# One weight preparation buffer, loaded and released in two halves of its columns

## The chip, the cores and the metric

The kernel runs on one core of a Trainium2 chip. The metric is the device time of one execution in microseconds; the kernel before took 2789.74 us (median of three runs). The engines are TensorE (PE, its weight loads shown as PEld), VectorE (DVE), ScalarE (ACT), GpSimd (POOL) and SyncE (SP), which issues most of the transfers.

## The reference

One layer of a hybrid decoder trunk over 2048 prompt tokens and 32 decoding tokens, in float32. Per token:

```
h = rmsnorm(x, g_mix_pre);  z = h @ w_in
a = z[value] * sigmoid(z[gate]) -> causal depthwise conv (31) -> group norm -> silu
hm = mlstm_chunkwise(q, k, v, i, f) -> per-head norm -> * sigmoid(z[o])
x = x + rmsnorm(concat(a, hm) @ w_out)
up = rmsnorm(x) @ w_up -> causal depthwise conv (3)
f = gelu(up[:, :D_FF]) * up[:, D_FF:]
x = x + rmsnorm(f @ w_down)
x = x + (p @ w_ple) * sigmoid(rmsnorm(x) @ w_ple_gate)
```

The model is 1024 wide, the feed-forward part 2816. The outputs are x and the states of the two convolutions and of the recurrence.

## The kernel before

The 2080 tokens are worked on in five blocks of 416. Features lie on the 128 partitions, tokens on the free dimension. Every product is made in three TensorE passes: a weight is kept as a high part (float32r) and a low part (the float32 value minus the high part), the activations likewise, and a 128x128 tile of weights costs `hi*hi`, `hi*lo` and `lo*hi` (lines 641 to 643), each 416 columns wide.

The weights are cut into 108 **units** of 128 x 1024 float32 values (512 KB). A unit serves 8 tiles, so 24 matmuls. In block 0 each unit is prepared once:

1. SP loads it raw into one of two buffers `w_raw[:, r % 2, :]` (`load_raw`, L522).
2. ACT copies it to the high part of `w[:, u % 3, 0, :]` (`high_part`, L1017). It does so inside its own fixed order of work, right after it has taken the result of the matmul group that used up unit u - 3 out of PSUM (`split_next`).
3. POOL subtracts to make the low part (`low_part`, L625). For 19 of the units VectorE does it (L2230, and L1808 for the first), in its own fixed order.
4. SP waits for that subtraction (`split_done`), loads the next raw unit but one into the buffer, and stores the finished pair of parts (1 MB) to the scratch tensor `w_kept` (`keep`, L529). The store must be complete before ACT writes that slot of `w` again (`s_kept`).

Blocks 1 to 4 only load finished pairs from `w_kept`; they have no raw loads, no copies and no POOL work. `w` is a ring of three slots, so TensorE can be at most two finished units ahead of the one in work. Each raw buffer has one counter `s_raw[i]` (a transfer adds 16), the high parts one counter `s_hi` (1 per unit), each slot of `w` one counter `s_w` (16 per unit, either from the subtraction or from a load).

Every engine runs a list of instructions in a fixed order. Around the change ACT's list for a pair j of up-projection groups in block 0 is: take group 2j out (L1398), split, GELU of pair j - 1 (L1406), take group 2j+1 out (L1398), split, high part of `f` for pair j - 1 (L1410). VectorE's is: `gated` (L2216), low part of `f` (L2220), the width-3 convolution of pair j (L2189, L2192), a copy of its tail (L2204), taps of the next block's width-31 convolution (L1722). The down projection (`f_split` as input) starts once the low parts of `f` are there. L1605 makes low parts of normalised activations, L1612 the scaled activations, L1600 sums squares, L2264 the low part of `p`, L806 begins a head of the recurrence after ACT's `columns` (L1126 to L1131).

Of the kernel before, what the change touches and what calls it, by code (L numbers as in the profile page):

```python
# [7 lines left out]
ALU = mybir.AluOpType  # L8
ACT = mybir.ActivationFunctionType
F32 = mybir.dt.float32  # L10
# [4 lines left out]
P = 128  # L15
D = 1024
KD = D // P
# [26 lines left out]
UNITS = 108  # L44
# [5 lines left out]
RAW = 2  # L50
RING = 3
# [104 lines left out]
def split_at(r):  # L156


    return SPLIT_UNITS[r]
# [26 lines left out]
def stores_before(u):  # L186


    return sum(split_at(r) % RING == u % RING and split_at(r) < u for r in range(SPLITS))
# [79 lines left out]
def hymba_layer(nc, t):  # L269
    ctx = ExitStack()  # L270
    with ctx:
# [3 lines left out]
        def signal(name, per, ring=0, unit=1):  # L275
            return Signal(ctx.enter_context(nc.semaphore(name)), per, ring, unit)
# [7 lines left out]
        w = sb("w_split", [P, RING, 2, KD * P], F32R)  # L284
        wg = sb("wg_split", [P, 2, KD, GATES], F32R)
        w_raw = sb("w_raw", [P, RAW, KD * P])
# [116 lines left out]
        s_setup = signal("s_setup", 0)  # L403
        s_ready = signal("s_ready", 0)
        s_gate_hi = signal("s_gate_hi", 0)
        s_raw = [signal(f"s_raw{i}", UNITS // RAW, unit=16) for i in range(RAW)]
        s_hi = signal("s_hi", UNITS)
        s_w = [signal(f"s_w{i}", UNITS // RING, unit=16) for i in range(RING)]
        s_kept = [signal(f"s_kept{i}", 0, unit=16) for i in range(RING)]
# [94 lines left out]
        def _(sp):  # L504
# [8 lines left out]
            def split_done(r):  # L513

                u = split_at(r)
                sp.wait_ge(s_w[u % RING].sem, s_w[u % RING].done(0, u // RING + 1))

            def load_raw(r):

                if r >= RAW:  # L520
                    split_done(r - RAW)
                sp.dma_start(w_raw[:, r % RAW, :], t["w_units"][source_of(split_at(r), False)]).then_inc(  # L522
                    s_raw[r % RAW].sem, 16)

            def keep(r):

# [91 lines left out]
        @block.gpsimd  # L618
        def _(pool):

            def low_part(n, r):

                slot = split_at(r) % RING
                pool.wait_ge(s_hi.sem, n + 1)
                nc.gpsimd.tensor_tensor(w[:, slot, 1, :], w_raw[:, r % RAW, :], w[:, slot, 0, :].bitcast(F32),  # L625
                                        ALU.subtract).then_inc(s_w[slot].sem, 16)

            for r in range(1, SPLITS):
                if r not in SPLIT_ON_VECTOR:
                    low_part(r, r)  # L630
# [374 lines left out]
        def _(act):  # L1005
# [5 lines left out]
            def high_part(u):  # L1011

                r = SPLIT_NTH[u]
                act.wait_ge(s_raw[r % RAW].sem, 16 * (r // RAW + 1))
                if u >= RING:
                    act.wait_ge(s_kept[u % RING].sem, 16 * stores_before(u))
                fn(w[:, u % RING, 0, :], w_raw[:, r % RAW, :], ACT.Copy).then_inc(s_hi.sem, 1)  # L1017

            def split_next(blk, split, g):

# [512 lines left out]
        def _(dve):  # L1533
# [22 lines left out]
            def program(blk, last, next_last=False, first=False, opening=False):  # L1556
# [247 lines left out]
                if first:  # L1804
                    sum_squares(0, range(KD))
                    inverse_root(0)
                    dve.wait_ge(s_hi.sem, 1)
                    v.tensor_tensor(w[:, 0, 1, :], w_raw[:, 0, :], w[:, 0, 0, :].bitcast(F32),  # L1808
                                    ALU.subtract).then_inc(s_w[0].sem, 16)
                    dve.wait_ge(s_rb.sem, s_rb.done(blk, 1))  # L1810
                    for i in range(KD + 4):
                        if i < KD:
# [410 lines left out]
                def low_part(u):  # L2223


                    if not opening or SPLIT_NTH.get(u) not in SPLIT_ON_VECTOR:
                        return
                    r, slot = SPLIT_NTH[u], u % RING
                    dve.wait_ge(s_hi.sem, r + 1)
                    v.tensor_tensor(w[:, slot, 1, :], w_raw[:, r % RAW, :], w[:, slot, 0, :].bitcast(F32),  # L2230
                                    ALU.subtract).then_inc(s_w[slot].sem, 16)

                def low_parts(g):
                    for u in USED_UP[False][g]:
# [212 lines left out]
```

## Time and profile before

| | |
|---|---|
| median of 3 runs | 2789.74 us (2786.82 to 2790.58) |
| the profiled execution | 2787.83 us, of which the traced span is 2785.8 us |
| PE, PEld busy | 97%, 94% of the span |
| DVE, ACT, POOL busy | 61%, 33%, 8% |
| mean granted TensorE clock | 0.994 of full speed |
| block 0 | about the first 665 us; all raw loads lie between 2.9 and 647.7 us |

A matmul takes about 350 ns from start to end but the next one starts about 189 ns later, since they are pipelined. So a busy PE of 97% hides small gaps; they are seen as idle time before a weight load (PEld). In the profile's tables the number in square brackets behind an instruction is the idle time of its engine just before it, with what ended it.

### The profile page before, as it was taken

How to read it: one execution, taken by the hardware profiler on the slowest of the kernel's cores; microseconds unless marked ns; L12 is line 12 of the kernel's file. 1: busy time of each engine (PE TensorE's matmuls, PEld its weight loads, DVE VectorE, ACT ScalarE, POOL GpSimd, SP SyncE). 2: the span in 40 equal slices, each digit the busy share in tenths (PEclk: the TensorE clock that was granted, in tenths of full speed). 3: DMA queues.
4: the chain of work that ended last, by engine and by line, in shares of the span. 5: the costliest groups of instructions: out<-in, count | busy, mean ns of one | idle time of the engine just before them, and what ended most of it. 6: DMA issues, size and time to landing. Idle time of an engine off the chain costs nothing.

```text
span 2785.8 us, 37566 instructions
## 1 busy us (share of the span) xinstructions
PE 2714.9 (97%) x14703; PEld 2610.3 (94%) x14703; DVE 1701.8 (61%) x3663; ACT 911.2 (33%) x1839; POOL 220.7 (8%) x92
## 2 busy tenths in 40 slices
PE   9989999999999999999999999999999999899998
PEld 7879999988899999999999999899999998799998
DVE  6976687765746756545566654656766636472644
ACT  5354433443532122434321223433112425211113
POOL 3421524311000000000000000000000000000000
PEclk9999999999999999999999999999999999999999
DMA  8747899978356666564666666556666576366665
GB/s 310 295 156 278 318 322 351 327 254 321 137 218 243 231 236 227 211 255 175 226 235 231 228 228 234 209 207 226 229 231 232 211 275 145 144 240 234 230 230 194
DMA packets 109562, 660.57 MB, mean 237 GB/s; under 512 B 20282, under 2 KB 20926, under 8 KB 39630
## 3 DMA queue, kind: packets, MB, share of 16 engines
q1 hardware_dynamic: 100238, 628.84, 63.2%
q10 hardware_dynamic: 9152, 29.36, 2.8%
q8 instruction: 117, 1.92, 0.3%
q14 instruction: 55, 0.45, 0.0%
HBM read 533.04 MB, written 125.11 MB: 236 GB/s over the span
## 4 chain that ended last, share of the span: by engine, by line
PE 77%; DMA 7%; DVE 7%; ACT 5%; POOL 2%; issue 1%; POOLq 0%; SPq 0%; DVEq 0%; ACTq 0%
PE proj L641 24%; PE proj L642 23%; PE proj L643 23%; DMA w_raw<-in_w_units 6%; POOL w_split L625 2%; ACT w_split L1017 2%; DVE mix_room L1600 1%; DVE small L1851 1%; DMA w_split<-w_kept 1%; PE m L679 1%; PE m L812 1%; DVE temp_room L1880 1%; PE m L818 1%; PE m L847 0%; PE m L848 0%
## 5 line engine op out<-in xcount | busy, mean ns | idle before, releaser
L641 PE MATMUL proj<-h_split,w_split 128*128 128x416 f32 x2720 | 977.8, 360 | 11.6 <-DVE h_split L1679 3.1
L642 PE MATMUL proj<-h_split,w_split 128*128 128x416 f32 x2720 | 954.0, 351 | 0.0
L643 PE MATMUL proj<-h_split,w_split 128*128 128x416 f32 x2720 | 948.4, 349 | 0.0
L641 PE MATMUL proj<-f_split,w_split 128*128 128x416 f32 x1568 | 566.0, 361 | 23.3 <-DVE f_split L1899 7.6
L642 PE MATMUL proj<-f_split,w_split 128*128 128x416 f32 x1568 | 553.7, 353 | 0.0
L643 PE MATMUL proj<-f_split,w_split 128*128 128x416 f32 x1568 | 550.1, 351 | 0.0
L641 PEld LDWEIGHTS proj<-h_split,w_split 128*128 128x128 f32 x2720 | 510.9, 188 | 25.6 <-issue 8.2
L643 PEld LDWEIGHTS proj<-h_split,w_split 128*128 128x128 f32 x2720 | 512.0, 188 | 8.7
L642 PEld LDWEIGHTS proj<-h_split,w_split 128*128 128x128 f32 x2720 | 512.5, 188 | 2.8 <-issue 1.0
L641 PEld LDWEIGHTS proj<-f_split,w_split 128*128 128x128 f32 x1568 | 297.1, 189 | 43.2 <-DVE f_split L1899 11.8
L643 PEld LDWEIGHTS proj<-f_split,w_split 128*128 128x128 f32 x1568 | 297.9, 190 | 5.3
L642 PEld LDWEIGHTS proj<-f_split,w_split 128*128 128x128 f32 x1568 | 298.0, 190 | 1.2
L1722 DVE SCALAR_TENSOR_TENSOR cv<-a_ext,vecs,cv 128x416 f32<-128x416 f32 (+1 forms) x480 | 289.7, 652 | 0.0
L2192 DVE SCALAR_TENSOR_TENSOR m<-temp_room,vecs,m 128x416 f32<-128x416 f32 (+1 forms) x440 | 256.8, 652 | 0.0
L625 POOL TENSOR_TENSOR w_split<-w_raw,w_split 128x1024 fp32r<-128x1024 f32 x88 | 220.5, 2507 | 436.4 <-ACT w_split L1017 436.4
L1398 ACT ACTIVATE temp_room<-proj 128x416 f32<-128x416 f32 x176 | 90.9, 517 | 470.7 <-PE proj L643 470.5
L2220 DVE TENSOR_TENSOR f_split<-m,f_split 128x416 fp32r<-128x416 f32 x110 | 65.1, 592 | 262.6 <-ACT f_split L1410 262.6
L2189 DVE TENSOR_SCALAR m<-temp_room,vecs 128x416 f32<-128x416 f32 (+1 forms) x220 | 146.1, 710 | 67.4 <-ACT temp_room L1398 66.5
L1017 ACT ACTIVATE w_split<-w_raw 128x1024 fp32r<-128x1024 f32 x108 | 114.1, 1057 | 145.3 <-DMA w_raw<-in_w_units 145.2
L1600 DVE TENSOR_TENSOR mix_room<-mix_room,temp_room 128x416 f32<-128x416 f32 x131 | 83.2, 635 | 109.5 <-ACT temp_room L1035 105.4
L1406 ACT ACTIVATE mix_room<-m 128x416 f32<-128x416 f32 (+1 forms) x110 | 57.2, 520 | 191.3 <-DVE m L2192 191.2
L1117 ACT ACTIVATE qkv<-proj 128x416 f32<-128x416 f32 x60 | 30.9, 515 | 167.8 <-PE proj L643 167.8
(284 smaller groups left out, 2226.1 us busy)
## 6 DMA issues: line engine op xcount, KB each, us to landing
w_split<-w_kept SPq DMA_DIRECT2D x432, 1024.0 KB, 4.8
w_kept<-w_split SPq DMA_DIRECT2D x108, 1024.0 KB, 7.7
w_raw<-in_w_units SPq DMA_DIRECT2D x108, 512.0 KB, 5.6
x_resid<-in_x ACTq DMA_DIRECT2D x5, 1664.0 KB, 12.5
out_y<-x_resid ACTq DMA_DIRECT2D x8, 832.0 KB, 8.9
rows<-in_x ACTq DMA_DIRECT2D x4, 832.0 KB, 8.2
w_raw<-in_x ACTq DMA_DIRECT2D x3, 832.0 KB, 11.9
qkv<-in_p ACTq DMA_DIRECT2D x5, 416.0 KB, 5.3
```

What stands on the lines that cost most here:

```text
L625: nc.gpsimd.tensor_tensor(w[:, slot, 1, :], w_raw[:, r % RAW, :], w[:, slot, 0, :].bitcast(F32), ALU.subtract).then_inc(s_w[slot].sem, 16)
L641: mm(dst, w_hi, a_hi, start=first, stop=False)
L642: mm(dst, w_hi, a_lo, start=False, stop=False)
L643: return mm(dst, w_lo, a_hi, start=False, stop=last)
L1017: fn(w[:, u % RING, 0, :], w_raw[:, r % RAW, :], ACT.Copy).then_inc(s_hi.sem, 1)
L1398: fn(s[:, n, 2:2 + T], src, ACT.Copy).then_inc(s_evac.sem, 1)
L1406: fn(gelu_out[:, j % 3, 0:wide], facc[j % 3][0][:, 0:wide], ACT.Gelu_apprx_tanh).then_inc(s_fgelu.sem, 1)
L1600: v.tensor_tensor(sq_sum, none if i == 1 else sq_sum, tile, ALU.add).then_inc(s_squse.sem, 2 if i == 1 else 1)
L1722: ins = v.scalar_tensor_tensor(acc[:, 0:n], a_ext[:, c, k:k + n], wt, acc[:, 0:n], ALU.mult, ALU.add)
L2189: ins = v.tensor_scalar(dst, src, wt, col("b_conv_ffn", n * FT + j), ALU.mult, ALU.add)
L2192: ins = v.scalar_tensor_tensor(dst, src, wt, dst, ALU.mult, ALU.add)
L2220: v.tensor_tensor(f[:, j % FH, 1, :], facc[j % 3][1][:, 0:T], f[:, j % FH, 0, :].bitcast(F32), ALU.subtract).then_inc(s_f.sem, 1)
```

## The change

The 1024 columns of a raw unit are treated as two halves of 512. Each half has its own load (256 KB), its own counter per raw buffer, its own ACT copy and its own subtraction on POOL or VectorE. A half of the raw buffer is loaded again once the subtraction of that half has been done: `s_w` now gets 8 from each half, and SP waits for the first 8 before the first half's load and for all 16 before the second's. The store of a finished unit and TensorE's wait for it still ask for both halves.

```diff
-        s_raw = [signal(f"s_raw{i}", UNITS // RAW, unit=16) for i in range(RAW)]
+        s_raw = [[signal(f"s_raw{i}_{part}", UNITS // RAW, unit=16) for part in range(2)] for i in range(RAW)]
+        raw_parts = (slice(0, KD * P // 2), slice(KD * P // 2, KD * P))
...
             def load_raw(r):
-                if r >= RAW:
-                    split_done(r - RAW)
-                sp.dma_start(w_raw[:, r % RAW, :], t["w_units"][source_of(split_at(r), False)]).then_inc(
-                    s_raw[r % RAW].sem, 16)
+                for part, cols in enumerate(raw_parts):
+                    if r >= RAW:
+                        u = split_at(r - RAW)
+                        sp.wait_ge(s_w[u % RING].sem, s_w[u % RING].done(0, u // RING + 1) - (0 if part else 8))
+                    sp.dma_start(w_raw[:, r % RAW, cols], t["w_units"][source_of(split_at(r), False)][:, cols]).then_inc(
+                        s_raw[r % RAW][part].sem, 16)
...
             def low_part(n, r):
                 slot = split_at(r) % RING
-                pool.wait_ge(s_hi.sem, n + 1)
-                nc.gpsimd.tensor_tensor(w[:, slot, 1, :], w_raw[:, r % RAW, :], w[:, slot, 0, :].bitcast(F32),
-                                        ALU.subtract).then_inc(s_w[slot].sem, 16)
+                for part, cols in enumerate(raw_parts):
+                    pool.wait_ge(s_hi.sem, 2 * n + part + 1)
+                    nc.gpsimd.tensor_tensor(w[:, slot, 1, cols], w_raw[:, r % RAW, cols], w[:, slot, 0, cols].bitcast(F32),
+                                            ALU.subtract).then_inc(s_w[slot].sem, 8)
...
             def high_part(u):
                 r = SPLIT_NTH[u]
-                act.wait_ge(s_raw[r % RAW].sem, 16 * (r // RAW + 1))
-                if u >= RING:
-                    act.wait_ge(s_kept[u % RING].sem, 16 * stores_before(u))
-                fn(w[:, u % RING, 0, :], w_raw[:, r % RAW, :], ACT.Copy).then_inc(s_hi.sem, 1)
+                for part, cols in enumerate(raw_parts):
+                    act.wait_ge(s_raw[r % RAW][part].sem, 16 * (r // RAW + 1))
+                    if u >= RING and part == 0:
+                        act.wait_ge(s_kept[u % RING].sem, 16 * stores_before(u))
+                    fn(w[:, u % RING, 0, cols], w_raw[:, r % RAW, cols], ACT.Copy).then_inc(s_hi.sem, 1)
```

The subtractions on VectorE (L1808, L2230) are split in the same way.

## Rows read from the trace of the kernel before

**Rows 1.** Instructions on the raw buffer, whole execution: count, ns min/median/max, first and last start.

```profile
L522 SPq DMA_DIRECT2D w_raw<-in_w_units x108: 327/333/718, 2.9 to 647.7; - x108
L1017 ACT ACTIVATE w_split<-w_raw x108: 1039/1060/1065, 10.9 to 653.6; 128x1024 fp32r<-128x1024 f32 x108
L625 POOL TENSOR_TENSOR w_split<-w_raw,w_split x88: 2357/2412/3934, 16.1 to 654.8; 128x1024 fp32r<-128x1024 f32 x88
...
L2230 DVE TENSOR_TENSOR w_split<-w_raw,w_split x19: 1215/1225/1233, 383.9 to 572.0; 128x1024 fp32r<-128x1024 f32 x19
...
  ACT w_split L1017: 145.2, 63
...
DMA to landing us min/median/max: 3.3/5.7/12.1
```

**Rows 2.** Chain that ended last, 320 to 340 us: start, length, what.

```profile
321.20 6.22 DMA w_raw<-in_w_units
...
327.45 1.07 ACT w_split L1017
...
328.65 2.42 POOL w_split L625
```

**Rows 3.** Busy time by stretch: two of block 0, one of a later block.

```profile
284.00:370.00 86.00, 85.60 (x451) 83.83 (x451) 55.91 (x96) 36.74 (x64) 44.42 (x18) 1.00 0.94 336
440.00:525.00 85.00, 84.84 (x447) 83.05 (x445) 60.09 (x98) 35.23 (x63) 43.48 (x19) 1.00 0.95 337
1000.00:1100.00 100.00, 99.95 (x530) 98.70 (x529) 63.59 (x122) 24.18 (x57) 0.00 (x0) 1.00 0.65 231
```

**Rows 4.** Weight loads with idle time before them, near the two down projections.

```profile
375.38 0.19 PEld L641 LDWEIGHTS proj<-f_split,w_split 128*128 128x128 f32 x1 [1.15 <-POOL w_split L625]
...
377.74 0.19 PEld L641 LDWEIGHTS proj<-f_split,w_split 128*128 128x128 f32 x1 [1.88 <-DVE f_split L2220]
...
525.42 0.19 PEld L641 LDWEIGHTS proj<-f_split,w_split 128*128 128x128 f32 x1 [0.68 <-issue]
...
532.77 0.19 PEld L641 LDWEIGHTS proj<-f_split,w_split 128*128 128x128 f32 x1 [2.32 <-DVE f_split L2220]
```

**Rows 5.** ACT in order of time, 375 to 377 us.

```profile
375.60 1.06 ACT L1017 ACTIVATE w_split<-w_raw 128x1024 fp32r<-128x1024 f32 x1 [1.99 <-DMA w_raw<-in_w_units]
376.56 0.50 ACT L1410 ACTIVATE f_split<-m 128x416 fp32r<-128x416 f32 x1
```

**Rows 6.** PE by stretch: busy, granted clock, DMA share, GB/s.

```profile
375.00:380.00 5.00, 3.10 (x12) 0.86 0.91 311
380.00:385.00 5.00, 5.00 (x23) 0.80 1.01 374
```

**Rows 7.** All engines in order of time, 267.9 to 270.9 us.

```profile
267.98 2.36 POOL L625 TENSOR_TENSOR w_split<-w_raw,w_split 128x1024 fp32r<-128x1024 f32 x1 [2.12 <-ACT w_split L1017]
...
268.09 2.70 DVE L1605 TENSOR_TENSOR h_split<-temp_room,h_split 128x416 fp32r<-128x416 f32 x1
...
270.84 0.19 PEld L641 LDWEIGHTS proj<-h_split,w_split 128*128 128x128 f32 x1 [2.22 <-DVE h_split L1605]
```

**Rows 8.** All engines in order of time, 605 to 609.4 us.

```profile
605.02 0.59 DVE L1600 TENSOR_TENSOR mix_room<-mix_room,temp_room 128x416 f32<-128x416 f32 x1
605.49 2.36 POOL L625 TENSOR_TENSOR w_split<-w_raw,w_split 128x1024 fp32r<-128x1024 f32 x1 [4.09 <-ACT w_split L1017]
...
605.82 2.48 DVE L1600 TENSOR_TENSOR mix_room<-mix_room,temp_room 128x416 f32<-128x416 f32 x1 [0.20 <-ACT temp_room L1035]
...
609.29 0.19 PEld L641 LDWEIGHTS proj<-f_split,w_split 128*128 128x128 f32 x1 [3.28 <-DVE f_split L2264]
```

**Rows 9.** ACT and PEld in order of time, 93 to 96.4 us.

```profile
93.19 1.06 ACT L1017 ACTIVATE w_split<-w_raw 128x1024 fp32r<-128x1024 f32 x1 [2.54 <-DMA w_raw<-in_w_units]
...
96.14 0.10 PEld L806 LDWEIGHTS m<-mask_b,sel_b 128*128 128x128 bf16 x1 [1.50 <-ACT small L1131]
```

**Rows 10.** DMA packets, 284 to 370 us and 1000 to 1100 us.

```profile
DMA packets 5284, 28.88 MB, mean 336 GB/s; under 512 B 591, under 2 KB 591, under 8 KB 2935
...
DMA packets 3173, 23.14 MB, mean 231 GB/s; under 512 B 352, under 2 KB 352, under 8 KB 352
```

**Rows 11.** Landing of the stores to `w_kept`, 280 to 540 us.

```profile
DMA to landing us min/median/max: 6.1/7.7/10.0
```

More of the change, by code:

```diff
@@ L1806, in program @@
                     inverse_root(0)
-                    dve.wait_ge(s_hi.sem, 1)
-                    v.tensor_tensor(w[:, 0, 1, :], w_raw[:, 0, :], w[:, 0, 0, :].bitcast(F32),
-                                    ALU.subtract).then_inc(s_w[0].sem, 16)
+                    for part, cols in enumerate(raw_parts):
+                        dve.wait_ge(s_hi.sem, part + 1)
+                        v.tensor_tensor(w[:, 0, 1, cols], w_raw[:, 0, cols], w[:, 0, 0, cols].bitcast(F32),
+                                        ALU.subtract).then_inc(s_w[0].sem, 8)
                     dve.wait_ge(s_rb.sem, s_rb.done(blk, 1))
@@ L2228, in low_part @@
                     r, slot = SPLIT_NTH[u], u % RING
-                    dve.wait_ge(s_hi.sem, r + 1)
-                    v.tensor_tensor(w[:, slot, 1, :], w_raw[:, r % RAW, :], w[:, slot, 0, :].bitcast(F32),
-                                    ALU.subtract).then_inc(s_w[slot].sem, 16)
+                    for part, cols in enumerate(raw_parts):
+                        dve.wait_ge(s_hi.sem, 2 * r + part + 1)
+                        v.tensor_tensor(w[:, slot, 1, cols], w_raw[:, r % RAW, cols], w[:, slot, 0, cols].bitcast(F32),
+                                        ALU.subtract).then_inc(s_w[slot].sem, 8)
                 def low_parts(g):
```

## The prediction

> **What bounds the kernel now.** I read the page first: PE is the bound, and its idle time is a few per cent. The change acts only on block 0, so the second look is at the raw buffers there. All 108 loads, 108 ACT copies and 88 POOL subtractions lie in the first 655 us, and ACT spends 145.2 us waiting for raw loads [rows 1]. That number is no gain by itself: ACT is not the bound.
>
> Third, the chain that ended last. One lap of one raw buffer is load 6.22, ACT 1.07, a gap of 0.13, POOL 2.42 [rows 2]. With the median load of 5.7 us [rows 1] a lap is 5.7 + 1.07 + 0.13 + 2.42 = 9.3 us. Two buffers make two units in a lap, 4.7 us each. TensorE wants one per 24 matmuls. In a later block, where nothing is split, 530 matmuls start in 100 us, 188.7 ns apart [rows 3], so a unit is due every 4.53 us. The preparation is slower than TensorE by some 0.15 us a unit, and the ring of three slots is used up slowly.
>
> Fourth, what that costs TensorE, since only this is worth anything. In 284 to 370 us 451 matmuls take 86 us where 451 x 0.1887 = 85.1 would do: 0.9 us lost. In 440 to 525 us 447 take 85 us instead of 84.3: 0.7 us [rows 3]. The larger losses come at the ends of the two up projections, when the ring is empty: idle times of 1.15, 1.88, 0.68 and 2.32 us [rows 4]. The one of 1.88 is "DVE f_split", but DVE got its input late from ACT: the copy of L1410 stood in ACT's order behind the raw unit's copy, which had waited 1.99 us for its load [rows 5]. Behind these idle times the granted clock is 0.86 and then 0.80 over 5 us each [rows 6]. Of the two levels, 2.4 and 1.2 GHz, the lower one then held for (0.14 + 0.20) x 2 x 5 = 3.4 us, which loses 1.7 us of work.
>
> Fifth, a second way in which the same instructions cost time. A DVE subtraction that takes 0.58 us elsewhere took 2.70 us: it began 0.11 us after a POOL subtraction and ended when that one had; TensorE waited 2.22 us for it [rows 7]. It happened again at 605.82, ahead of an idle time of 3.28 us; the same form had taken 0.59 us just before [rows 8]. And once ACT's wait for a raw load delays the start of a head, 1.50 us of TensorE [rows 9].
>
> **The change part by part.**
>
> *The lap.* A half's own lap is load + half an ACT copy + gap + half a subtraction. No row shows the half sizes. ACT's lies between 0.53 and 1.06 us; the next ACT instruction starts 0.96 after one of 1.06 [rows 5], so some 0.1 is a tail, and I take 0.6. POOL's lies between 1.2 and 2.4; I take 1.3, near proportional, as the nearest row has only the one size. The load of 256 KB lies between 5.7 (nothing saved) and 5.7 - 0.78 = 4.9 us (262144 bytes at 336 GB/s [rows 3] less); I take 5.3. Lap: 5.3 + 0.6 + 0.13 + 1.3 = 7.3 us for two units, 3.7 each (3.5 to 3.9). That is below 4.53, so the preparation is no longer slower than TensorE. Even a POOL half of 2.4 us would only make POOL about even (4.8 a unit).
>
> *What ends last then.* Not SP: its 108 more issues of 0.33 us [rows 1] are 36 us of an idle queue; queued behind each second-half wait are the store and the next load, which both waited for the same event before. Not the slot: a store lands in 7.7, at most 10.0 us [rows 11]. It is issued some 4 us after ACT began, so the slot is free at 11.7 (14.0 at worst) against 3 x 4.53 = 13.6 us. Rarely late, and the stores start no later than now.
>
> *The DMA engines.* This is the tight one. 28.88 MB in 86 us are 18.4 units (1.573 MB each: the load and the store), at a share of 0.94: 4.40 us of DMA time per unit. At TensorE's pace that is a share of 0.97. The change adds per unit 128 data packets and one small packet for each of the 16 engines: 591 small packets go with 37 transfers, 16 each [rows 10]. That is 9 packets more per engine. Their price from below: 0.94 x 86 x 16 / 28.88 = 44.8 us per MB with half the data packets of 4 KB, and 0.65 x 100 x 16 / 23.14 = 44.9 us per MB with 8 KB packets only. Smaller packets show no price. From above: a 2 KB packet could last as long as one of 4 KB, 0.18 us instead of 0.09, which is 9 x 0.09 = 0.8 us a unit. I take nothing, by the nearest row.
>
> The Trainium skill, Perfetto Trace Analysis, section DMA Optimizations, speaks against the change: it says that small transfers below 2 KB carry a notable overhead and that going from 2 KB to 4 or 8 KB can raise the throughput greatly when a kernel is bound by its DMAs. The profile's rows go down to 4 KB and show no price there, so whether it holds at 2 KB stays open. By another page, DMA: Bandwidth & Descriptors, section Why small descriptors are slow, the fixed part is about 3 cycles per packet at 850 MHz; nine of them would be an estimated 0.03 us a unit, and the sum would stay as it is.
>
> *The sum.* Gains, full and taken: the trickle in the two stretches 0.9 + 0.7, taken 1.4. The idle time on POOL at 375.38, 1.15, taken 1.1. The one at 377.74, 1.88, taken 1.5, as ACT no longer stands in a wait. The clock behind them 1.7, taken 1.2. At 525.42 0.68, taken 0.6. At 532.77 2.32, taken 1.0, since DVE itself was late there too. At 270.84 2.22, taken 1.8: with POOL's instruction half as long DVE waits 1.2 us less, and the first half ends before it. At 609.29, 3.28, taken 0.8 of it: a part of one blocked DVE instruction, the rest being DVE's own work. At 96.14 1.50, taken 1.0. Together 1.4 + 1.1 + 1.5 + 1.2 + 0.6 + 1.0 + 1.8 + 0.8 + 1.0 = 10.4 us. Losses: an ACT pair is about 0.1 us longer than one copy, hidden in ACT's idle time (33% busy), and a DVE pair, 19 times, likewise about 0.1 over 1.225 us [rows 1]. Where DVE's or ACT's chain is what TensorE waits for, I count 0.6 in all. Net 9.8 us, less than 1% of block 0's 665 us. Blocks 1 to 4 are untouched.
>
> The profiled execution took 2787.83 us (span 2785.8, 2.0 around it), 1.9 below the median of the runs. It would take 2778.0; on the median 2789.74 - 9.8 = 2779.9, and I say 2780.
>
> **The rivals.**
>
> *A, packets.* Slower. The raw loads of 2 KB rows make the DMA engines the bound. The preparation now takes 86 / 18.4 = 4.67 us a unit. With c per added packet the DMA engines need 4.40 + 9c. This passes the pace of today at c = 30 ns. Over the 44 units of the two up projections, and with the gains outside them (1.8 + 0.8 + 1.0 = 3.6) kept, it is slower than before by over 5.6 us from c = 53 ns: (9c - 0.27) x 44 = 9.2. At 70 ns: (0.63 - 0.27) x 44 - 3.6 = 12 us, 2802. At the upper bound of 90 ns, 20 us, 2810. For it: DMA shares of 0.94 and 0.95 [rows 3], so nothing hides it. Against it: no price at 4 KB [rows 10]. The skill's page on traces named above is the rule behind it.
>
> *B, the laps are not what TensorE waits for.* The idle times at the ends come from DVE's and ACT's own chains, or the second half lands as late as the whole did (its load is issued at the same moment as now, and the queue ahead of it is the same). Then only the trickle and parts of the POOL effect are won, 2 to 4 us: 2786 to 2788. For it: at 532.77 ACT's wait alone doesn't explain 2.32 us. Against it: rows 5, where the wait is plainly in front.
>
> *C, two locks for one.* POOL's halves run back to back, and DVE's next two instructions are each caught by one instead of one by the whole. Then the 1.8 and 0.8 turn into nothing, and DVE's list in the up projections loses a little: 9.8 - 2.6 - 1 = 6 us gained, 2784; with a loss at DVE's chain of more than 6 us it would be no gain. The Trainium skill, SBUF — State Buffer, states that a DVE instruction with two SBUF inputs and a GpSimd one that reads SBUF exclude each other for a whole instruction; rows 7 agree.
>
> **How the numbers follow.** A measurement of this kernel can tell about 0.2%, 5.6 us, from no change. Chances: the forecast (7 to 14 us gained) 0.53, A 0.12 (of it 0.09 slower by over 5.6), B 0.20, C 0.15. Faster by over 0.2%: the forecast and half of C, 0.60. Within: B, half of C less a little, and the mild part of A, 0.29. Slower: A's strong part and a remainder of C, 0.11. The full gains with no loss are 1.6 + 1.15 + 1.88 + 1.7 + 0.68 + 2.32 + 2.22 + 0.8 + 1.5 = 13.9, and if all of 609.29 went too, 16.3: low end 2773. The high end takes in B and the mild part of A: 2791. The likeliest case alone spans 2776 to 2783.
>
> **What the profile after would show.** Right: ACT's wait for raw loads far below 145 us; 530 matmuls per 100 us in the stretches of rows 3; no idle of 1.15 and 1.88 us before the first down projection and a clock of 1.00 behind it; POOL halves of 1.2 to 1.4 us; DVE subtractions of at most about 1.8 us where one took 2.70; DMA share 0.97. Wrong: a DMA share of 0.97 or more with a pace below that of rows 3 and loads that land later than 5.7 us (A); ACT's waits gone but the idle times of rows 4 still there (B); pairs of DVE instructions of 1.7 us each (C). A POOL half well above 1.3 us would make the lap wrong, and the prediction with it from 2.3 us on.

## The result, and the profile after

The changed kernel takes **2764.69 us** (median of 3, 2764.65 to 2767.98) against 2789.74 before: a ratio of 0.9904, interval 0.9887 to 0.992. That is 25 us on the medians and 19.8 on the profiled executions (2787.83 to 2767.98). The forecast was 2780 with a range down to 2773, so the direction was right, the time lies below the range, and the gain came out at twice its size or more. Measured again later, the same two kernels took 2765.89 and 2790.32: ratio 0.991, interval 0.9897 to 0.9924.

The instructions on the raw buffer after, as in [rows 1]:

```profile
L525 SPq DMA_DIRECT2D w_raw<-in_w_units x216: 327/328/1449, 2.8 to 625.8; - x108
L1022 ACT ACTIVATE w_split<-w_raw x216: 612/623/635, 10.5 to 632.0; 128x512 fp32r<-128x512 f32 x108
L629 POOL TENSOR_TENSOR w_split<-w_raw,w_split x176: 1268/1301/3256, 14.7 to 633.5; 128x512 fp32r<-128x512 f32 x176
L2237 DVE TENSOR_TENSOR w_split<-w_raw,w_split x38: 678/684/693, 373.4 to 555.6; 128x512 fp32r<-128x512 f32 x38
...
  ACT w_split L1022: 6.7, 10
...
DMA to landing us min/median/max: 2.5/4.6/12.4
```

The step sizes came out as forecast: ACT's half 0.62 (0.6 taken), POOL's 1.30 (1.3). The load lands in 4.6 us, below the 4.9 that I gave as its lowest. ACT's wait for raw loads fell from 145.2 us to 6.7. The stretches of [rows 3]:

```profile
284.00:370.00 86.00, 86.00 (x457) 85.11 (x456) 73.05 (x106) 38.48 (x84) 48.44 (x38) 1.00 0.96 359
440.00:525.00 85.00, 85.00 (x452) 84.14 (x451) 72.51 (x105) 37.09 (x80) 44.58 (x35) 1.00 0.93 344
```

457 matmuls in 86 us are 188.2 ns apart, the pace of a later block. Where the time came from is seen when the up and down projection are cut up further. Before:

```profile
250.00:300.00 50.00, 47.96 (x256) 46.17 (x256) 26.59 (x42) 21.55 (x36) 19.44 (x8) 1.00 0.70 254
...
350.00:400.00 50.00, 47.22 (x237) 44.94 (x236) 42.81 (x69) 18.01 (x29) 16.06 (x7) 0.97 0.92 320
...
500.00:550.00 50.00, 47.45 (x246) 45.09 (x245) 35.66 (x61) 20.29 (x35) 18.54 (x8) 1.00 0.93 331
550.00:584.00 34.00, 30.90 (x161) 29.63 (x160) 23.10 (x37) 14.23 (x23) 0.00 (x0) 1.00 0.90 328
```

After:

```profile
250.00:300.00 50.00, 49.93 (x265) 48.56 (x264) 31.87 (x48) 25.21 (x50) 25.95 (x20) 1.00 0.79 294
...
350.00:400.00 50.00, 49.97 (x265) 49.09 (x265) 46.83 (x79) 18.03 (x36) 10.35 (x9) 1.00 0.89 324
...
500.00:550.00 50.00, 49.95 (x265) 49.10 (x264) 43.50 (x74) 23.31 (x48) 10.28 (x9) 1.00 0.87 323
550.00:584.00 34.00, 32.14 (x175) 30.93 (x174) 19.69 (x35) 15.12 (x28) 3.88 (x3) 1.00 0.82 285
```

The matmul counts rise by 9, 28, 19 and 14, together 70, and 70 x 0.1887 = 13.2 us. The three stretches that are not shown (300 to 350, 400 to 450, 450 to 500) had 266 or 267 matmuls in 50 us already before. So in this execution nothing was lost in the middle of a projection; the loss sat where one ends and the next begins. The clock of 0.97 is 1.00 after.

That is the rule and not without exception. In two more profiles of the kernel before, the first stretch of [rows 3] loses nothing (457 matmuls from 284 to 370 us), but in one of them the second does, by a single idle time of 1.73 us at 487.65:

```profile
440.00:525.00 85.00, 82.46 (x431) 79.85 (x430) 54.05 (x99) 33.73 (x62) 44.28 (x18) 1.00 0.93 327
```

This table cuts all profiled executions at the same instructions (first matmul of a head, L812 before; first matmul of a norm's sum, L679 before). The column "falls" is the work that TensorE lost from 90 to 690 us by the granted clock, read in stretches of 5 us and divided by 1.7 us: it came out as a whole number each time, within 0.2. A long fall counts for two, as the one from 605 to 625 us before, which is shown further down. The names of the kernels are those of the next section.

| kernel | execution | to first head | to up projection | up and down | to block 1's first head | rest | falls |
|---|---|---|---|---|---|---|---|
| before | 2787.8 | 96.5 | 153.2 | 335.1 | 94.8 | 2106.2 | 5 |
| before, second profile | 2792.5 | 96.9 | 154.4 | 339.6 | 93.3 | 2106.3 | 7 |
| before, third profile | 2794.0 | 94.3 | 155.3 | 339.1 | 95.2 | 2108.0 | 9 |
| after | 2768.0 | 94.0 | 153.5 | 320.9 | 89.9 | 2107.8 | 2 |
| after, second profile | 2770.5 | 95.4 | 153.7 | 323.7 | 87.9 | 2107.9 | 3 |
| only compute in halves | 2778.0 | 94.7 | 158.4 | 327.4 | 89.9 | 2105.8 | 3 |
| only loads in halves | 2794.3 | 96.0 | 157.3 | 333.3 | 96.7 | 2108.9 | 6 |
| loads and ACT in halves | 2782.1 | 94.3 | 156.6 | 325.1 | 96.1 | 2108.0 | 4 |
| only POOL in halves | 2789.4 | 97.7 | 156.0 | 336.4 | 91.1 | 2106.5 | 5 |
| after, whole release | 2766.2 | 95.3 | 152.7 | 320.4 | 91.2 | 2104.6 | 2 |
| quarters | 2769.7 | 94.4 | 152.0 | 321.6 | 89.2 | 2110.7 | 2 |
| third buffer | 2776.7 | 94.1 | 152.2 | 324.5 | 91.7 | 2112.1 | 4 |
| third buffer, halves | 2770.4 | 94.4 | 152.9 | 320.3 | 89.3 | 2111.7 | 2 |
| third buffer, late state load | 2770.5 | 94.3 | 153.1 | 323.0 | 91.9 | 2106.2 | 3 |
| the same, second profile | 2775.6 | 94.1 | 154.0 | 327.7 | 91.4 | 2106.4 | 3 |
| the same, third profile | 2769.9 | 94.2 | 152.1 | 324.7 | 91.9 | 2105.0 | 4 |
| the same, fourth profile | 2771.1 | 94.0 | 152.9 | 323.0 | 94.0 | 2105.1 | 3 |
| late state load, with halves | 2766.1 | 94.3 | 152.5 | 320.2 | 89.4 | 2107.9 | 2 |

### The profile page after: what moved, and what is told of

It is laid out like the page before. It is cut to its first block, busy times and chain, and to the rows that moved or that the text cites. A ratio compares the mean times of both kernels' runs of the same rounds, so it can differ in the third digit from the quotient of the medians.

```text
span 2766.1 us, 37998 instructions
## 1 busy us (share of the span) xinstructions
PE 2707.4 (98%) x14703; PEld 2604.8 (94%) x14703; DVE 1707.8 (62%) x3683; ACT 921.5 (33%) x1947; POOL 241.1 (9%) x180
## 4 chain that ended last, share of the span: by engine, by line
PE 89%; DVE 6%; ACT 3%; DMA 2%; issue 1%; SPq 0%; DVEq 0%; ACTq 0%
PE proj L645 28%; PE proj L646 27%; PE proj L647 27%; DMA w_split<-w_kept 1%; DVE mix_room L1605 1%; DVE small L1857 1%; PE m L816 1%; DVE temp_room L1886 1%; PE m L683 1%; PE m L822 1%; PE m L851 1%; PE m L852 0%; DVE f_split L1905 0%; PE m L773 0%; PE m L645 0%
## 5 line engine op out<-in xcount | busy, mean ns | idle before, releaser
L1727 DVE SCALAR_TENSOR_TENSOR cv<-a_ext,vecs,cv 128x416 f32<-128x416 f32 (+1 forms) x480 | 305.7, 684 | 0.0
L1403 ACT ACTIVATE temp_room<-proj 128x416 f32<-128x416 f32 x176 | 91.2, 518 | 564.6 <-PE proj L647 564.5
L629 POOL TENSOR_TENSOR w_split<-w_raw,w_split 128x512 fp32r<-128x512 f32 x176 | 240.8, 1391 | 393.8 <-ACT w_split L1022 393.7
L1022 ACT ACTIVATE w_split<-w_raw 128x512 fp32r<-128x512 f32 x216 | 124.4, 624 | 7.1 <-DMA w_raw<-in_w_units 6.7
```

Source lines behind the costliest of these rows:

```text
L629: nc.gpsimd.tensor_tensor(w[:, slot, 1, cols], w_raw[:, r % RAW, cols], w[:, slot, 0, cols].bitcast(F32), ALU.subtract).then_inc(s_w[slot] ...
L1022: fn(w[:, u % RING, 0, cols], w_raw[:, r % RAW, cols], ACT.Copy).then_inc(s_hi.sem, 1)
L1403: fn(s[:, n, 2:2 + T], src, ACT.Copy).then_inc(s_evac.sem, 1)
L1727: ins = v.scalar_tensor_tensor(acc[:, 0:n], a_ext[:, c, k:k + n], wt, acc[:, 0:n], ALU.mult, ALU.add)
```

## The experiments

Theory L: the lap of a raw buffer (load, copy, subtraction) is longer than TensorE's pace allows, and the change shortens it. Theory P: what counts is that POOL's instruction is half as long, so that VectorE is caught by less of it. Theory A: the 2 KB rows of the half loads cost DMA time.

**Compute in halves, load and release whole** (against the kernel before):

```diff
 ...
+                for part, cols in enumerate(raw_parts):
+                    pool.wait_ge(s_hi.sem, 2 * n + part + 1)
+                    nc.gpsimd.tensor_tensor(w[:, slot, 1, cols], w_raw[:, r % RAW, cols], w[:, slot, 0, cols].bitcast(F32),
+                                            ALU.subtract).then_inc(s_w[slot].sem, 8)
 ...
+                for part, cols in enumerate(raw_parts):
+                    act.wait_ge(s_raw[r % RAW].sem, 16 * (r // RAW + 1))
 ...
```

> ACT and POOL or VectorE work in halves, but a raw unit is loaded by one transfer and its buffer is released when both halves are subtracted. Theory L (the lap of a raw buffer sets the time): the lap is 5.7 + 0.62 + 0.13 + 2.6 = 9.05 us against 9.3 before and 7.3 in the changed kernel, about TensorE's own pace of 9.06, so a third to a half of the gain: 2775 to 2783 us, ACT still waits tens of us for raw loads. Theory P (the shorter POOL instructions, which block VectorE for less time, give most of it): nearly the whole gain, 2765 to 2770 us.

2778.39 us, ratio 0.9948 (0.9935 to 0.9961): about half of the gain, as theory L expected; the 2765 to 2770 of theory P did not come. ACT still waited 146.8 us for raw loads, 68 times. The idle time of 2.22 us on VectorE's `h_split` [rows 7] is gone, the first of the stretches below runs at 49.92, but the ones in which the two down projections begin are not repaired (49.97 and 49.95 after):

```profile
250.00:300.00 50.00, 49.92 (x269) 48.53 (x268) 25.85 (x45) 24.27 (x47) 21.08 (x16) 1.00 0.73 259
350.00:400.00 50.00, 48.11 (x251) 46.09 (x250) 43.89 (x75) 19.24 (x39) 17.32 (x13) 1.00 0.90 320
500.00:550.00 50.00, 48.86 (x257) 47.49 (x256) 42.50 (x69) 23.60 (x50) 18.32 (x15) 1.00 0.97 342
```

**Loads in halves, all else whole:**

```diff
+                for part, cols in enumerate(raw_parts):
+                    sp.dma_start(w_raw[:, r % RAW, cols], t["w_units"][source_of(split_at(r), False)][:, cols]).then_inc(
+                        s_raw[r % RAW][part].sem, 16)
 ...
+                for part in range(2):
+                    act.wait_ge(s_raw[r % RAW][part].sem, 16 * (r // RAW + 1))
```

> Only the transfers are halved: two loads of 256 KB with a counter each, both issued when the whole unit is subtracted; ACT waits for both and copies the whole, POOL subtracts the whole. Theories L and P both expect no gain: 2788 to 2792 us. If 2 KB packets or the extra transfers have a price on the DMA engines (c per added packet, 9 per engine and unit), the raw loads land later than 5.7 us and the time is above: 30 ns each would give some 10 us, 2800 us.

2788.88 us, ratio 0.9982 (0.9973 to 0.9991). Theory A is refuted: with every raw load in 2 KB rows the kernel isn't slower, and in the changed kernel the DMA share from 284 to 370 us is 0.96 at 359 GB/s against 0.94 at 336 [rows 3], 43 us of DMA time per MB and engine sum (0.96 x 86 x 16 / 30.86) against 44.8:

```profile
DMA packets 8390, 30.86 MB, mean 359 GB/s; under 512 B 929, under 2 KB 929, under 8 KB 5860
```

ACT waited 152.5 us here, so earlier landing of the halves alone gives little: 0.2% on the medians, with an interval that just leaves out no change. The profiled execution, 2794.26 us, was the longest of eleven.

**Loads and ACT copies in halves, subtraction whole** (POOL waits for both copies with `pool.wait_ge(s_hi.sem, 2 * (n + 1))`):

> Loads and ACT copies in halves, POOL's and VectorE's subtraction whole and the buffer released whole. Theory L: the lap loses about 0.45 us of ACT's copy (the first half is copied while the second lands): 8.9 us, just under TensorE's 9.06, so a third to a half of the gain, 2776 to 2784 us. Theory P: POOL's instruction is as long as before, so no gain: 2786 to 2792 us.

2780.27 us, ratio 0.9949 (0.9937 to 0.9961): half of the gain with POOL's instruction as long as before, which theory P excluded. The lap is shorter by the copy that overlaps the second load: ACT waited 66.3 us. The two ends are repaired, while the 2.24 us on `h_split` at 272 us and the long last stage (96.1 us) stay, the reverse of the first experiment (last stage 89.9 us):

```profile
250.00:300.00 50.00, 47.85 (x248) 46.02 (x247) 27.79 (x41) 23.30 (x44) 19.11 (x8) 0.97 0.65 240
350.00:400.00 50.00, 49.95 (x265) 49.09 (x264) 45.46 (x71) 21.05 (x41) 14.45 (x6) 1.00 0.90 334
500.00:550.00 50.00, 49.95 (x265) 49.00 (x264) 36.92 (x62) 24.73 (x49) 15.26 (x6) 1.00 0.91 326
```

These three kernels also spent 78.3 to 79.4 us on the first three heads, against 74.7 in the first profile of before. In the one with halved loads VectorE's seven taps took 6.13 us behind a POOL subtraction (4.03 for the same form before), and TensorE waited 3.15 us for what follows:

```profile
144.31 6.13 DVE L1744 SCALAR_TENSOR_TENSOR cv<-a_ext,vecs,cv 128x416 f32<-128x416 f32 x7
150.37 0.57 DVE L1760 TENSOR_TENSOR cv<-cv,m 128x416 f32<-128x416 f32 x1
...
151.00 0.40 PEld L761 LDWEIGHTS m<-ident,cv 128*104 128x104 f32 x4 [3.15 <-DVE cv L1760]
```

The kernel with halved compute lost as much there. Its two POOL halves each caught one tap, so that two short blocks cost what one long one does (6.05 us for the seven taps):

```profile
142.81 6.05 DVE L1744 SCALAR_TENSOR_TENSOR cv<-a_ext,vecs,cv 128x416 f32<-128x416 f32 x7
...
144.81 3.04 POOL L627 TENSOR_TENSOR w_split<-w_raw,w_split 128x512 fp32r<-128x512 f32 x2 [5.06 <-ACT w_split L1020]
```

**POOL's subtraction alone in two instructions:**

```diff
+                for cols in (slice(0, KD * P // 2), slice(KD * P // 2, KD * P)):
+                    nc.gpsimd.tensor_tensor(w[:, slot, 1, cols], w_raw[:, r % RAW, cols], w[:, slot, 0, cols].bitcast(F32),
+                                            ALU.subtract).then_inc(s_w[slot].sem, 8)
```

> Only POOL's subtraction is cut in two, issued back to back after a whole ACT copy; loads, copies, VectorE's subtractions and the release are whole. The lap is not shorter (2.6 us of POOL instead of 2.4). Theory L+P (two effects, the lap in the up and down projections, POOL's blocking of VectorE at the end of the block): the up and down projections (335 us before) keep their time within 2 us, the end of block 0 (from the second norm sum to the next block's first head, 94.8 us before) loses about 5 us; in all 4 to 6 us under the kernel before. Theory L alone: no gain. Theory C (two locks for one): slower than before in the up projections by 2 us or more.

2796.14 us, ratio 1.001 (0.9996 to 1.0023): no gain, where theory L+P expected 4 to 6 us. The pair is 0.2 us longer than the whole (2 x 1.30 against 2.41), the lap with it, and ACT's wait rose to 173.5 us. The locked instruction of [rows 7] is gone (250 to 300 us: 49.70 busy) and the last stage is 3.7 us shorter, as L+P said; but up and down projection took 336.4 us instead of 335.1 in spite of the 2.2 us won there, so their ends are worse by about 3.5, and the stages ahead of them are longer too. The slower expected by theory C (2 us or more in the up projections) isn't told apart from the longer lap.

**The changed kernel with the early release undone** (both halves wait for all 16):

```diff
+                if r >= RAW:
+                    split_done(r - RAW)
 ...
-                    if r >= RAW:
-                        u = split_at(r - RAW)
-                        sp.wait_ge(s_w[u % RING].sem, s_w[u % RING].done(0, u // RING + 1) - (0 if part else 8))
```

> The changed kernel with one part undone: both loads of a unit wait for both halves of the old one. The lap is 4.7 + 0.78 for the second load's data, + 0.62 + 0.13 + 1.3 = about 7.5 to 8 us against TensorE's 9.06, so theory L expects nearly all of the gain without the early release: within 3 us of the changed kernel, 2765 to 2770 us. If the early release is what counts, it ends near the kernel with halved work and whole loads, 2778 us.

2765.41 us, ratio 0.9902 (0.9887 to 0.9917): the changed kernel. ACT's wait is 35.4 us instead of 6.7, and no TensorE time is seen to hang on it. The early release is slack.

**Quarters instead of halves** (`raw_parts` of four slices of 256 columns, counts of 4):

> Four parts of 256 columns instead of two of 512, in loads (128 KB, 1 KB rows), copies, subtractions and releases. Theory L: the lap was already below TensorE's pace with halves, so no more from it: 2763 to 2768 us. Theory P: POOL instructions of some 0.75 us block VectorE for less time again, 1 to 3 us better than the halves: 2761 to 2764 us. If small packets have a price, it shows here first: over 2770 us, with a higher DMA share for the same bytes.

2767.68 us, ratio 0.9909 (0.9896 to 0.9922), no more and no less than halves. A POOL quarter takes 0.74 us and an ACT quarter 0.41: 2.97 and 1.62 us a unit, against 2.60 and 1.25 in halves. Rows of 1 KB have no price either (a share of 0.98 at 355 GB/s from 284 to 370 us). The 2761 to 2764 of theory P did not come, although VectorE stood behind POOL for much less time: counting every VectorE instruction of block 0 that lasted over 0.2 us more than the median of its line, the time beyond that median is 49 us with quarters, 74 with halves and 73 in the first profile of before.

**A third raw buffer in the kernel before**, all instructions whole. Its room is that of `a_dec`, whose load moves behind block 1:

```diff
-RAW = 2
+RAW = 3
 ...
+        raw_third = a_dec[:, :, :, :].rearrange("p c b e -> p (c b e)")[:, 0:KD * P]
```

> The kernel before with a third raw buffer (in the room of the decoding tokens' convolution window, whose state is loaded after block 1 instead of at the start); everything else whole. The lap stays 9.3 us but makes three units, 3.1 us each. Theory L+P: ACT's wait for raw loads goes from 145 us to under 20, the up and down projections lose 12 to 14 us as in the changed kernel, and the end of block 0 keeps its 95 us, since POOL's instruction is as long as before: 2775 to 2780 us. Theory P alone: no gain, 2790 us.

> The changed kernel with the third raw buffer as well. Theory L+P: the lap was no longer what TensorE waits for, so nothing is left to win from it: 2763 to 2768 us, the same as the changed kernel within 3 us. More than 4 us under it would mean that raw loads still held it back.

2782.27 us, ratio 0.9958 (0.9943 to 0.9973), and with halves 2771.08, ratio 0.9924 (0.991 to 0.9939). ACT waited for no raw load at all in either, though the loads of 5.8 us landed no sooner. The first of the two times is above the 2775 to 2780 that L+P expected. Block 0 ended 17.1 us sooner in the profiled execution, against 21.3 us after the change. The idle time from [rows 7] is still there with whole subtractions:

```profile
264.47 2.36 POOL L630 TENSOR_TENSOR w_split<-w_raw,w_split 128x1024 fp32r<-128x1024 f32 x1 [2.12 <-ACT w_split L1022]
...
264.58 2.69 DVE L1614 TENSOR_TENSOR h_split<-temp_room,h_split 128x416 fp32r<-128x416 f32 x1
```

Both lost some 4 us later ("rest" of 2112 in the table). That is the moved load, see the last section. So I moved it on to block 2:

```diff
+                        if blk == 2:
+                            for n in range(RING):
+                                act.wait_ge(s_w[n].sem, s_w[n].done(0, UNITS // RING + FRONT // RING))
+                            act.dma_start(state_homes[1][1], t["a_dec"]).then_inc(s_states.sem, 16)
```

> The kernel before with a third raw buffer and whole instructions. The room is that of the decode gates' state, whose load moves to block 2, where DMA and ACT have time. Theory L: two buffers were the fault, so the third recovers most, without halves: block 0 ends 17 us sooner, as in the experiment with the load in block 1, and blocks 1 and 2 are as before; 14 to 19 us under the kernel before. Theory P (shorter POOL instructions do the main part): at most 8 us under it. Both: VectorE's subtractions of over 2.4 us behind one of POOL's stay, and the stage after the down projection keeps 91 to 94 us.

> The changed kernel with a third raw buffer on top, state load as in the run before. Theory L: with halves the lap is already below TensorE's pace (ACT waits 6.7 us for raw loads in the whole run), so a third buffer adds nothing: within 3 us of the changed kernel, and 3 to 9 us under the kernel with a third buffer and whole instructions, the part that POOL's length costs. If halves and a third buffer each removed a part of the lap's cost, it would be over 5 us under the changed kernel.

> The changed kernel, unchanged, in more rounds and with a second profile, beside the last two kernels on the same chip. Theory L (the lap of a raw buffer) and theory P (the length of POOL's instruction) both expect the difference measured before, 0.9904 within 0.002, that is 22 to 29 us; stages of block 0 as in the first profile within 1 us: 74.4 over three heads, 320.8 over up and down projection, 89.9 to the end of the block.

> The kernel before, unchanged, with a second profile. It tells whether the 3.6 to 4.7 us that three experiments lost over the first three heads (78.3 to 79.4 us against 74.7) belong to those kernels or to the kernel before as well. If POOL's whole or half instruction catches VectorE's taps there by chance of the alignment (theory P), this profile may show either 74.7 or about 78.5 us over those three heads; up and down projection of block 0 stay at 335 us within 1.5, by either theory. If the loss belongs to the experiments' own edits, it shows 74.7 again. Time: within 0.2% of the kernel before.

On one chip: third buffer 2778.04, ratio 0.9957 (0.9944 to 0.9971); third buffer and halves 2766.62, 0.9918 (0.9904 to 0.9931); the changed kernel 2765.89, 0.991 (0.9897 to 0.9924); the kernel before 2793.07 in ten runs beside 2790.32 in fifteen, 1.0007 (0.9994 to 1.002). With halves a third buffer adds nothing. With whole instructions it gives 12.3 of 24.4 us on the medians, less than the 14 to 19 that theory L expected; but its profiled execution took 2770.48 while the other four took 2777.5 to 2781.5. To see where these lie, it was profiled three times more, and the kernel before once:

> The kernel with a third raw buffer and whole instructions once more, for a second profile. Its executions took 2770.5 (profiled), 2777.5, 2778.0, 2778.3 and 2781.5 us. Theory T (taps): an execution of 2777 or more has 78 to 79 us over the first three heads, with an idle time of TensorE of about 3 us on VectorE's taps near 150 us, and one of about 2771 has 74.7. Theory R (ring): the 7 us lie in up and down projection, 330 us instead of 323, at 74.7 over the heads.

> The same kernel, third profile: as for the run before it, by the time that it takes. Theory T: 2777 or more with 78 to 79 us over three heads, or 2771 with 74.7. Theory R: the difference in up and down projection.

> The same kernel, fourth profile: as for the two runs before it. Should all three profiles fall at 2771 us, neither theory is told apart, and the difference between profile and median stays open.

> The kernel before, third profile. Its executions took 2786 to 2802 us; profiles so far 2787.8 and 2792.5, with 74.7 and 76.1 us over three heads and 335.1 and 339.6 in up and down projection. Theory T: an execution over 2793 has 78 us or more over three heads. Theory R: it has over 339 in up and down projection, as the second profile had, with single lost waits of about 1.7 us on the ring.

They took 2775.57, 2769.87 and 2771.05, and before 2793.97. All three have 74.7 us over the heads, so theory T found no support in this kernel; but none of them took 2777 or more, so it isn't refuted either. The one of 2775.57 has its extra time in up and down projection (327.7 us against 323.0), where theory R put it. Most of it is not idle time: the same idle time is followed by a fall of the clock in one execution and not in another. The two executions of the third-buffer kernel, 2770.48 first:

```profile
265.00:280.00 15.00, 13.09 (x68) 11.95 (x67) 10.60 (x16) 5.59 (x11) 5.62 (x3) 1.00 0.60 210
```

```profile
265.00:280.00 15.00, 13.10 (x59) 11.94 (x60) 9.09 (x14) 6.03 (x11) 3.37 (x2) 0.89 0.64 224
```

PE is equally busy in both (13.09 and 13.10), with 68 matmuls at a clock of 1.00 and 59 at 0.89: nine matmuls, 1.7 us. A second such fall at 570 us makes 3.4 of the 4.7 us. The rest is the idle time before the stage's last groups, 2.55 us against 0.93; the trace shows nothing that ended the longer one. The clock explains this stage only: over block 0 both executions have 3 falls (the other had its own at other places), and the 5.1 us between them are then idle time. In the third profile of before the same is seen at the idle times of [rows 4], 0.77 where [rows 6] and its neighbours made 0.89, and once more at 530 us, where the first profile had 1.00:

```profile
370.00:385.00 15.00, 12.39 (x50) 11.37 (x49) 9.41 (x19) 5.31 (x8) 4.73 (x2) 0.77 0.86 332
530.00:545.00 15.00, 12.44 (x57) 11.47 (x56) 9.59 (x18) 5.70 (x9) 2.37 (x1) 0.89 0.84 304
```

So before had 5, 7 and 9 falls of 1.7 us in block 0, and after 2 and 3: on average 4.5 fewer, which is 7.7 us of work.

## Why the prediction was right in sign and wrong in size

**What held.** The bound (TensorE, late by its waits), the lap as the cause, the sizes of the halves and the pace of the two stretches came out as forecast. ACT's idle time was indeed in the way: with a third buffer alone the ends are repaired. Rival A did not come: no packet price at 2 KB or 1 KB.

Rival C came in its mechanism and not at its price. POOL's halves run back to back and each catches a VectorE instruction: before, 43 of VectorE's instructions in block 0 were over 0.2 us longer than the median of their line, after 84, and the time beyond the median is no shorter (73 us before and 74 after; 66 and 68 in the two other profiles of before, 73 in the other of after). Where TensorE had waited 2.22 us [rows 7], one pair of halves caught two subtractions, for 1.14 and 1.00 us instead of 0.58 each (the second stands in the group of four, which would take 2.08 alone). That is 1.0 us for both where the whole cost 2.1:

```profile
265.93 1.14 DVE L1610 TENSOR_TENSOR h_split<-temp_room,h_split 128x416 fp32r<-128x416 f32 x1
...
267.67 2.51 DVE L1610 TENSOR_TENSOR h_split<-temp_room,h_split 128x416 fp32r<-128x416 f32 x4
```

```profile
265.32 2.90 POOL L629 TENSOR_TENSOR w_split<-w_raw,w_split 128x512 fp32r<-128x512 f32 x2 [1.62 <-ACT w_split L1022]
```

At the end of the block, where [rows 8] had 2.48 us and then 1.01 for `f_split`, the halves won nothing for VectorE: 1.32 and 2.09 us, together 1.8 us too long against 1.9.

```profile
588.14 3.30 POOL L629 TENSOR_TENSOR w_split<-w_raw,w_split 128x512 fp32r<-128x512 f32 x2 [2.10 <-ACT w_split L1022]
```

```profile
588.99 1.32 DVE L1605 TENSOR_TENSOR mix_room<-mix_room,temp_room 128x416 f32<-128x416 f32 x1 [0.30 <-ACT temp_room L1040]
590.23 2.09 DVE L2271 TENSOR_TENSOR f_split<-qkv,f_split 128x832 fp32r<-128x832 f32 x1
```

Rival B (the second half lands no sooner, the ends are DVE's and ACT's own) fell with the idle times of [rows 4], of which not one is left. VectorE's and ACT's lateness there was not their own: both stood behind the unit's copy and its subtraction. Ahead of the idle time of 2.32 us at 532.77, before the change, a VectorE copy of 4 columns lasted 2.26 us beside a POOL subtraction, and ACT's raw copy, with the high part of `f` behind it, waited 2.36 us for its load:

```profile
527.04 2.40 POOL L625 TENSOR_TENSOR w_split<-w_raw,w_split 128x1024 fp32r<-128x1024 f32 x1 [1.69 <-ACT w_split L1017]
...
527.22 2.26 DVE L2204 COPY up_tail<-temp_room 128x4 f32<-128x4 f32 x1
...
530.63 1.06 ACT L1017 ACTIVATE w_split<-w_raw 128x1024 fp32r<-128x1024 f32 x1 [2.36 <-DMA w_raw<-in_w_units]
```

**What failed: the sum.** Its terms, on the first two profiles:

| part of block 0 | taken | measured |
|---|---|---|
| to the first head (at 96.14: 1.0) | 1.0 | 2.5 |
| up and down projection: 1.4 + 1.1 + 1.5 + 1.2 + 0.6 + 1.0 + 1.8 | 8.6 | 14.2 |
| behind it (at 609.29: 0.8) | 0.8 | 4.9 |
| elsewhere, losses | -0.6 | -1.8 |
| sum | 9.8 | 19.8 |

The up and down projection fell short in two ways. First, I discounted: the rows that I had named are worth 0.9 + 0.7 + 1.15 + 1.88 + 1.7 + 0.68 + 2.32 + 2.22 = 11.6 us, and all of it came in this pair of executions (the 0.9 and 0.7 by luck in part, as other profiles of before show less or more of them). The largest discount was "at 532.77 2.32, taken 1.0, since DVE itself was late there too". Second, I left out what no row that I had read showed: between 540 and 584 us two idle times of 1.08 and 2.66 us. The first is gone after, the second is 1.16 (565.42 below), which makes the other 2.6 us. An idle time of 1.33 follows in the next stage, which begins at 568.4, and is new:

```profile
565.42 0.19 PEld L645 LDWEIGHTS proj<-h_split,w_split 128*128 128x128 f32 x1 [1.16 <-ACT temp_room L1446]
...
572.33 0.19 PEld L645 LDWEIGHTS proj<-h_split,w_split 128*128 128x128 f32 x1 [1.33 <-ACT sig_o L1063]
```

Behind the projections the term "At 609.29, 3.28, taken 0.8 of it" named one idle time and forgot the clock behind it and the idle times that follow. From 605 to 625 us the clock was 0.83, which is 0.17 x 20 = 3.4 us of work; after, 0.91:

```profile
605.00:625.00 20.00, 17.11 (x79) 15.51 (x78) 10.71 (x14) 10.29 (x19) 5.25 (x3) 0.83 0.46 158
```

```profile
605.00:625.00 20.00, 17.80 (x85) 16.80 (x84) 14.14 (x16) 13.00 (x21) 11.55 (x8) 0.91 0.59 209
```

The idle time itself fell from 3.28 to 1.91 us. The reason that the term gave, a blocked VectorE instruction that gets shorter, failed there, as the rows above show; what shortened it is not shown. Two later idle times are POOL's instruction in plain sight. The first waits for VectorE's low parts, of which POOL caught one:

```profile
625.45 2.11 DVE L1605 TENSOR_TENSOR f_split<-temp_room,f_split 128x416 fp32r<-128x416 f32 x1
...
627.61 0.19 PEld L641 LDWEIGHTS proj<-f_split,w_split 128*128 128x128 f32 x1 [1.37 <-DVE f_split L1605]
```

```profile
605.11 1.01 DVE L1610 TENSOR_TENSOR f_split<-temp_room,f_split 128x416 fp32r<-128x416 f32 x1
...
607.77 0.19 PEld L645 LDWEIGHTS proj<-f_split,w_split 128*128 128x128 f32 x1 [0.45 <-DVE f_split L1610]
```

In all ten profiles with whole subtractions it is 1.35 to 1.46 us, in all eight with halves or quarters at most 0.54. The second (2.86 at 636.12) is 2.86 or 2.87 in the ten and 2.45 or less in the eight. An idle time of 1.47 at 664.72 is gone as well, while the one of 1.33 came in. All idle time of this stage together fell by 3.2 us and the clock's loss by 1.7, which is the 4.9.

For the first part, the idle time of 1.50 is gone and the rest is better supply in front of it (13 to 50 us: clock 0.95 instead of 0.91); it is not all the change's, as the third profile of before reached the first head at 94.3 too. The -1.8 elsewhere is not the loss of 0.6 that I counted: 1.6 of it lies behind block 0, and one more fall of the clock there (0.97 instead of 0.98 from 2300 to 2450 us) is worth 1.7.

**The rest of the miss, from 19.8 to 25 us,** is the choice of base. I took the profiled execution as typical, but it had the fewest falls of the clock of three (5, 7, 9). By the mean of all profiles of these two kernels the gain is 2791.4 - 2769.3 = 22.1 us, of it 7.7 by the clock, for which the sum had 1.2; the medians say 24 to 25.

**How the gain divides.** Averaged over its five profiles the third buffer alone brings up and down projection to 324.6 us, from 337.9 over three profiles of before: 13.3 us for the lap. Halves on top bring 320.2: 4.4 more, and in the stage behind it 92.2 becomes 89.4. Halves are worth that where the lap doesn't bind; POOL's halves alone gave nothing. How much of it is POOL's shorter instruction isn't fully told apart, since there the loads and ACT's copies are halved too: the idle times that go with its length alone, in every profile, are 2.2 us at [rows 7], 0.9 and 0.4 at the end of the block. On the medians the part of the whole instructions looks larger (2778.04 against 2766.62, 11.4 us). The four profiled executions of the third-buffer kernel with the late state load took 2769.9 to 2775.6, on average 2771.7, and explain about 5 of these 11 us; what the unprofiled executions of 2777.5 to 2781.5 us lose is not seen and stays open. The taps that POOL caught in three other kernels (3.6 to 4.7 us) would do a part of it, but no profile of this one shows them.

## What to carry to other kernels

Where a producer's lap is some 3% too slow for a ring of three slots, the loss shows mostly at the seams between phases: there each late instruction of one engine also delays the next phase's inputs on others. Such idle times share one cause; count them in full, add the clock behind each, and list all seams before summing. Splitting a stage into halves cures a lap as well as a further buffer does, without its room. It does not block a second engine at a shared port for less time in all, since each half catches an instruction; it helps at those places where one block of full length stood before TensorE. Before a difference is set against a median, take the profile of the kernel before more than once.

## What the runs showed of the hardware

**With the raw loads split, other transfers landed sooner.** With raw loads in 2 KB rows the stores to `w_kept`, still of 4 KB and more, landed in 6.5 us (5.5 to 9.0 from 280 to 540 us) instead of 7.7 [rows 11]; with halved loads alone 6.9, with halved compute alone 7.9, and with quarters 5.7. Whether it is the shorter rows or the smaller transfers was not separated. The Trainium skill, Perfetto Trace Analysis, section DMA Optimizations, says that transfers under 2 KB carry a notable overhead and that splitting may help if the DMA engines are generally idle. Read as a statement on rows, the first did not hold here: 1 KB rows had no price. The condition of the second was not needed: the engines had a share of 0.94, and the split load landed sooner.

**Two instructions queued on POOL don't keep VectorE out.** In none of the profiles was a VectorE instruction longer than its usual time by more than one of POOL's, even with two of POOL's queued; the second half of a pair waits in its turn (2.90 us for the pair of 1.30 each). The Trainium skill, SBUF — State Buffer, section Who interferes with whom, states that the lock is exclusive for a whole instruction; the lengths of 2.69 us beside a whole subtraction and 1.00 to 1.14 beside a half agree.

**Behind a transfer in very small rows the next issue can last long.** Behind the moved load of `a_dec` (480 KB in rows of 120 bytes, issued at 1183.22) ACT's next DMA issue lasted 7.37 us, where the same line had taken 0.35; in the kernel with halves it was 7.32. ACT's later work stood behind it, and TensorE waited 4.03 us. That it is the rows, and not the size or the place, is not shown:

```profile
1190.37 7.37 ACTq L1251 DMA_DIRECT2D rows<-in_x  x1
...
1198.27 0.52 ACT L1122 ACTIVATE qkv<-proj 128x416 f32<-128x416 f32 x1 [5.88 <-issue]
```

```profile
1198.83 0.81 PEld L817 LDWEIGHTS m<-qkv 128*104 128x104 f32 x8 [4.03 <-ACT qkv L1122]
```

Moved behind a step of block 2, where ACT issues no transfer soon after it, the same load cost nothing ("rest" 2106.2).

**A fall of the clock is not certain behind an idle time.** Behind the same 2.2 us of idle TensorE it came in some executions and not in others, each time at 1.7 us of lost work. The spread is narrower after the change too, 2764.9 to 2770.5 in five executions against 2786.4 to 2801.6 in fifteen before; that fewer idle times are the reason was not tested.
